# New PSUM banks and a new gate order in the first stage, and whole float32 copies for the 16-column products

## The reference, cut to what matters

```python
# first block (x is 512 x 1024, c is one condition vector)
sh1, sc1, g1, sh2, sc2, g2 = split(silu(c) @ ada_w + ada_b)      # ada_w is 1024 x 6144
u = rms_norm(x, mix_pre_g) * (1 + sc1) + sh1
y = concat_g((window_mean(u_g, w_g) - u_g) @ pool_w[g]) * pool_scale   # 4 groups of 256 columns
x = x + g1 * rms_norm(y, mix_post_g)
u = rms_norm(x, ffn_pre_g) * (1 + sc2) + sh2
x = x + g2 * rms_norm(conv_ffn(u), ffn_post_g)                   # u @ w_up (1024 x 5632), conv, gelu, @ w_down
# second block: two layers
p = x @ w_in                # gdn: q, k, v, gate, and 16 columns of b and a logits
x = layer_norm(a * x + gated_delta_rule(...) @ w_out)
p = x @ w_in                # gla: q, k, v, gate, and 16 columns of low rank gate input
x = layer_norm(a * x + gla_chunked(...) @ w_out)
```

## Time and profile before

| | |
|---|---|
| median of 3 runs | 1145.33 us (1144.76 to 1145.80) |
| profiled execution | 1145.01 us, span 1143.2 us |
| PE busy | 1123.7 us, 98% of the span |
| DVE, ACT, POOL busy | 548.4, 499.1 and 451.2 us |
| TensorE clock granted, mean | 0.996 of full speed |

### The profile page before, as it was taken

How to read it: one execution, slowest core, us unless ns; L and a number is a source line. 1 busy time by engine, 2 the same in 40 slices (tenths; PEclk the granted TensorE clock), 3 DMA queues, 4 the chain that set the end, 5 groups by cost and what they waited for, 6 DMA issues and landing times.

```text
span 1143.2 us, 17115 instructions
## 1 busy us (share of the span) xinstructions
PE 1123.7 (98%) x6826; PEld 916.5 (80%) x6826; DVE 548.4 (48%) x882; ACT 499.1 (44%) x692; POOL 451.2 (39%) x346
## 2 busy tenths in 40 slices
PE   8989999999999999999999999999999999999997
PEld 5658888888888888888788878888888888888886
DVE  3672554324452234567986556422200443676825
ACT  3374453544421223875443255744322343534632
POOL 0115544545445471654432211035354444564430
PEclk8999999999999999999999999999999999999999
DMA  9993232332342333433232211122343322223201
GB/s 343 415 384 111 74 110 82 101 110 73 110 128 78 111 111 112 148 110 112 75 108 78 75 37 38 74 74 74 108 125 109 111 79 91 95 75 111 75 1 74
DMA packets 87240, 128.97 MB, mean 113 GB/s; under 512 B 13300, under 2 KB 66306, under 8 KB 86919
## 3 DMA queue, kind: packets, MB, share of 16 engines
q1 hardware_dynamic: 81730, 119.62, 31.0%
q10 hardware_dynamic: 5445, 8.42, 2.1%
HBM read 122.77 MB, written 5.26 MB: 112 GB/s over the span
## 4 chain that ended last, share of the span: by engine, by line
PE 85%; DVE 5%; issue 3%; DMA 2%; ACT 2%; SPq 1%; POOL 1%; DVEq 0%; POOLq 0%
PE ps L295 24%; PE ps L297 24%; PE ps L296 24%; PE ps L1804 3%; DVE conv_v L1339 2%; DMA ada<-in_ada_w 1%; PE ps L2344 1%; DVE diag L1389 1%; PE ps L2345 1%; PE ps L2413 1%; PE ps L2403 1%; POOL wl L443 1%; PE ps L2350 1%; DVE outer L1386 1%; DVE shift_acc L1107 1%
## 5 line engine op out<-in xcount | busy, mean ns | idle before, releaser
L443 POOL TENSOR_TENSOR wl<-raw,wh 128x512 fp32r<-128x512 f32 x312 | 420.5, 1380 | 612.5 <-ACT wh L494 612.5
L295 PE MATMUL ps<-xth,wh 128*128 128x512 f32 (+1 forms) x832 | 324.4, 390 | 1.8 <-DVE xtl L1236 1.4
L297 PE MATMUL ps<-xth,wl 128*128 128x512 f32 (+1 forms) x832 | 317.4, 382 | 0.0
L296 PE MATMUL ps<-xtl,wh 128*128 128x512 f32 (+1 forms) x832 | 317.3, 381 | 0.0
L494 ACT ACTIVATE wh<-raw 128x2048 fp32r<-128x2048 f32 x78 | 149.3, 1914 | 304.9 <-PE ps L297 284.7
L295 PEld LDWEIGHTS ps<-xth,wh 128*128 128x128 f32 x832 | 156.5, 188 | 34.6 <-issue 4.5
L297 PEld LDWEIGHTS ps<-xth,wl 128*128 128x128 f32 x832 | 156.4, 188 | 30.4
L296 PEld LDWEIGHTS ps<-xtl,wh 128*128 128x128 f32 x832 | 156.7, 188 | 28.7 <-issue 0.5
L1244 DVE SCALAR_TENSOR_TENSOR conv_out<-ps,conv_taps,conv_out 128x511 f32<-128x511 f32 x44 | 32.8, 745 | 124.8 <-ACT conv_out L665 124.8
L1339 DVE SCALAR_TENSOR_TENSOR conv_v<-ps,gdn_taps,conv_v 128x511 f32<-128x511 f32 (+2 forms) x96 | 71.8, 748 | 40.2 <-ACT conv_v L733 37.5
L295 PE MATMUL ps<-wh,xth 128*128 128x512 f32 x176 | 69.7, 396 | 0.0
(11 more groups left out here) (368 smaller groups left out, 1628.1 us busy)
## 6 DMA issues: line engine op xcount, KB each, us to landing
ada<-in_ada_w SPq DMA_DIRECT2D x24, 1024.0 KB, 12.8
raw<-in_gdn_w_in SPq DMA_DIRECT2D x24, 1024.0 KB, 5.2
raw<-in_ffn_w_up SPq DMA_DIRECT2D x22, 1024.0 KB, 4.9
raw<-in_gla_w_in SPq DMA_DIRECT2D x12, 1024.0 KB, 5.0
raw<-in_ffn_w_down SPq DMA_DIRECT2D x11, 1024.0 KB, 4.9
raw<-in_gdn_w_out SPq DMA_DIRECT2D x8, 1024.0 KB, 4.9
raw<-in_gla_w_out SPq DMA_DIRECT2D x4, 1024.0 KB, 5.1
xres<-in_x SPq DMA_DIRECT2D x4, 512.0 KB, 5.3
```

What stands on the lines that cost most here:

```text
L295: nc.tensor.matmul(o, lh, rh, start=first, stop=False)
L296: nc.tensor.matmul(o, lh, rl, start=False, stop=False)
L297: return nc.tensor.matmul(o, ll, rh, start=False, stop=last)
L443: rest = nc.gpsimd.tensor_tensor(lo[:, part], raw[:, s, part], hi[:, part].bitcast(f32), ALU.subtract)
```

## The change

In the first stage the banks of y rotate as 2, 4, 6, 2 where they were 4, 6, 2, 4, and those of the turned tiles as 4, 6, 2, 4 where they were 6, 2, 4, 6. The first y tile is copied by ACT into SBUF (`first_mixed`), so that DVE works on it there and tile 3 may take its banks. The order of the programs of PE, DVE and ACT changes with it, some waits are taken at other places, four products of ones are put between the vector rows, two behind `mod_col`, and the four ahead of the up projection go. The second half of the second gain is summed between the first channel tiles, and the up unit runs both its halves for each channel tile instead of four tiles at a time. In the two `first_unit` stages ACT writes a third copy of each turned tile, `xt_whole`, in plain float32, and `narrow` reads that alone. The diff, cut to its core:

```diff
+    xt_whole = [at("xt_gdn", PH + 72 * KB, [KD, T]), at("xt_gla", PH + 32 * KB, [KD, T])]
+    first_mixed = at("first_mixed", PH, [D])
...
         def mixed_bank(tt):
+            return (2, 4, 6, 2)[tt]
+        def turned_bank(tt):
             return (4, 6, 2, 4)[tt]
-        def turned_bank(tt):
-            return (6, 2, 4, 6)[tt]
...
 # ACT: parts_high
                 nc.scalar.activation(xth[:, :, tt * P:(tt + 1) * P], ..., ACT.Copy).then_inc(S("parts_hi"), 1)
+                if stage < 2:
+                    for half in (1, 0):
+                        if half == 0:
+                            act.wait_ge(S("parts_lo"), parts_count(stage, tt, 2) + 1)
+                        nc.scalar.activation(xt_whole[stage][:, 4 * half:4 * half + 4, tt * P:(tt + 1) * P],
+                                             ps[:, b + half, :]..., ACT.Copy).then_inc(S("parts_hi"), 1)
...
 # ACT: first stage
-            for tt in range(2):
-                norm_square("y", tt)
-                norm_root("y", tt)
+            norm_square("y", 0)
+            norm_root("y", 0)
+            act.wait_ge(S("pool_in"), 34)
+            nc.scalar.activation(first_mixed[:], bank2(mixed_bank(0)), ACT.Copy).then_inc(S("act_ready"), 1)
+            norm_square("y", 1)
+            norm_root("y", 1)
...
-            nc.scalar.activation(ada_part[:, 1, :], ps[:, 1, :], ACT.Copy).then_inc(S("ada_summed"), 1)
...
-            norm_scale(3)
...
+            act.wait_ge(S("turned"), 4)
+            nc.scalar.activation(pooled[:, 4:KD, 3 * P:T], ps[:, turned_bank(3) + 1, :]..., ACT.Copy)...
...
 # DVE: parts_low in two halves, each behind ACT's copy of the other half
+                if stage < 2:
+                    for half in range(2):
+                        v.wait_ge(S("parts_hi"), parts_count(stage, tt, 3) + 1 + half)
+                        V.tensor_tensor(xtl[:, k, cols], ps[:, b + half, :]..., xth[:, k, cols].bitcast(f32), ALU.subtract)...
...
 # DVE: first stage
             norm("y", 1)
+            v.wait_ge(S("vec_mm"), 3)
+            V.tensor_tensor(g1_row[:, 0:512], ps[:, 0, :], post1_row[:, 0:512], ALU.mult)...
             v.wait_ge(S("mod_mm"), 4)
-            V.tensor_tensor(g1_row[:], bank2(0), post1_row[:], ALU.mult)...
+            V.tensor_tensor(g1_row[:, 512:D], ps[:, 1, :], post1_row[:, 512:D], ALU.mult)...
...
             norm("u", 2)
+            ada_sum(3)
             turned_out(0)
             norm("u", 3)
+            V.tensor_scalar(xn[:, 3, :], xres[:, 3, :], stat[:, 2, 3:4], None, ALU.mult)...
             turned_out(1)
             gain_sum(0)
             mod_col(3, 1, SH2)
+            v.wait_ge(S("turned"), 4)
+            V.tensor_copy(pooled[:, 0:4, 3 * P:T], ps[:, turned_bank(3), :]...)...
             gain_col(0)
-            gain_sum(1)
-            turned_out(3)
...
+            modulated(2)
+            modulated_low(0)
+            modulated_low(1)
+            gain_sum(1)
+            modulated_low(2)
+            gain_col(1)
+            v.wait_ge(S("mods_done"), 6)
...
 # PE
                 mm.then_inc(S("vec_mm"), 1)
+                keep_busy(2, 5)
...
-            pe.wait_ge(S("vec_done"), 2)
-            for n in range(3):
-                ada_unit(1, n)
+            pe.wait_ge(S("vec_done"), 1)
+            ada_unit(1, 0)
+            ada_unit(1, 1)
             pool_block(0)
             pool_block(1)
+            ada_unit(1, 2)
+            pool_block(2)
+            pool_block(3)
             ada_unit(1, 3)
-            pool_block(2)
+            pe.wait_ge(S("vec_done"), 2)
             mod_col(1, 3, 0)
             mod_col(1, 3, 1)
-            for cb in range(3, KD):
-                pool_block(cb)
-            mixed(0)
+            keep_busy(2, 2)
+            pool_block(4)
+            pool_block(5)
+            mixed_group(0, 0)
+            pool_block(6)
+            mixed_group(0, 1)
+            pool_block(7)
+            mixed_group(0, 2)
+            mixed_group(0, 3)
             mixed(1)
+            mixed_group(2, 0)
+            mixed_group(2, 1)
...
             mixed_shift(0)
-            mixed_shift(1)
             ada_unit(2, 2)
             ada_unit(2, 3)
+            mixed_shift(1)
+            mod_row(2, 0)
             mixed_group(2, 2)
-            mod_row(2, 0)
             mixed_group(2, 3)
             mixed_shift(2)
+            mixed(3)
+            mixed_shift(3)
             ada_unit(3, 0)
             ada_unit(3, 1)
-            mixed(3)
-            mixed_shift(3)
+            turn_normed(0)
...
-            gain_turn(1)
-            pe.wait_ge(S("pooled_written"), 2)
-            keep_busy(4, 3)
...
-                for part in range(2):
-                    for sub in range(2):
+                for k in range(KD):
+                    if k == 2:
+                        gain_turn(1)
+                    pe.wait_ge(S("u_lo"), k + 1)
+                    for sub in range(2):
...
 # PE: narrow
-                    for x in (xth, xtl):
-                        for c in range(4):
-                            mm = X.matmul(ps[32 * c:32 * c + 32, b, cols], w[:, kk + c, :], x[:, kk + c, cols].bitcast(f32), ...)
+                    for c in range(4):
+                        mm = X.matmul(ps[32 * c:32 * c + 32, b, cols], w[:, kk + c, :], xt_whole[stage][:, kk + c, cols], ...)
```

More of the change, by code:

```diff
@@ L252, in cell_bank, with pool_bank, mixed_tile, gain_bank @@
             return (4, 5, 7)[m % 3]
+        def pool_bank(cb):
+            return 4 + (cb + 1) % 4
+        def mixed_tile(tt):
+            return first_mixed[:] if tt == 0 else bank2(mixed_bank(tt))
         def mixed_bank(tt):
+            return (2, 4, 6, 2)[tt]
+        def turned_bank(tt):
             return (4, 6, 2, 4)[tt]
-        def turned_bank(tt):
-            return (6, 2, 4, 6)[tt]
+        def gain_bank(half):
+            return (0, 6)[half]
+        def gain_cols_bank(half):
+            return (0, 7)[half]
+        def parts_count(stage, tt, each):
+            return each * (stage * TT + tt) if stage < 2 else each * 2 * TT + tt
         def keys_bank(c):
@@ L1227, in _, with modulated_low @@
             modulated(0)
[L1228 to L1236 removed]
+            def modulated_low(n):
+                v.wait_ge(S("pooled_done"), KD + n + 1)
+                V.tensor_tensor(xtl[:, n, :], pooled[:, n, :], xth[:, n, :].bitcast(f32), ALU.subtract).then_inc(S("u_lo"), 1)
+            modulated(2)
[5 more added lines that the diff above has]
+            v.wait_ge(S("mods_done"), 6)
+            modulated(4)
+            modulated_low(3)
+            modulated(6)
+            for n in range(4, KD):
+                modulated_low(n)
             def up_taps(i, s, sub):
@@ L1980, in _ @@
             ada_unit(2, 0)
-            mixed_group(2, 0)
             pe.wait_ge(S("mods_done"), 2)
@@ L2160, in turn_x3, with narrow @@
                 turn_tile(xres[:, tt, :], 2 * tt)
-            def narrow(b, w, part):
+            def narrow(b, w, stage, part):
                 cols = slice(part * 256, part * 256 + 256)
                 for kk in range(0, KD, 4):
-                    for x in (xth, xtl):
-                        for c in range(4):
-                            mm = X.matmul(ps[32 * c:32 * c + 32, b, cols], w[:, kk + c, :], x[:, kk + c, cols].bitcast(f32),
-                                          start=(kk == 0 and x is xth), stop=(kk > 0 and x is xtl))
+                    for c in range(4):
+                        mm = X.matmul(ps[32 * c:32 * c + 32, b, cols], w[:, kk + c, :], xt_whole[stage][:, kk + c, cols],
+                                      start=(kk == 0), stop=(kk > 0))
                 return mm
@@ L2179, in beta_gate @@
                     pe.wait_ge(S("padded"), 1)
-                mm = narrow(3, ba_w, part)
+                mm = narrow(3, ba_w, 0, part)
                 if part == 1:
@@ L2485, in gate_low @@
                     pe.wait_ge(S("padded"), 2)
-                mm = narrow(2, low_w, part)
+                mm = narrow(2, low_w, 1, part)
                 if part == 1:
```

103 lines of the change are left out of this document (51 added, 52 removed).

## The result

The changed kernel took 1150.74 us (median of 20 runs, 1145.60 to 1151.92) beside 1144.74 us (20 runs) of the kernel before: ratio 1.0043, 95% interval 1.0033 to 1.0052. Forecast were 1141.1 us and a range that ends at 1146.0. The 20 times form two groups, called heaps here: 8 lie at 1145.6 to 1148.0, 12 at 1150.6 to 1151.9. The mean granted clock is 0.992 to 0.995 in the first and 0.989 to 0.990 in the second; the runs of the kernel before have 0.993 to 0.999. The profiled execution took 1145.67 us with a span of 1143.9 and belongs to the lower heap.

What follows compares the result with a forecast made beforehand. PE, busy 98% of the span, was taken as the bound. First stage 1.7, stage 1 1.7 and stage 0 0.7 make 4.1 us below 1145.01, or 1140.9, forecast as 1141.1; 8-in-10 range 1138.9 to 1146.0.

Steps and rivals of the forecast that it cites:

- The clock between 15 and 22 us: First stage: the clock stays high, so gate units start at 18.7 us; taken as little better than even.
- The price of splitting the pairs: First stage: products of ones end the pairs' overlap, each pair 1.8 us; gate units start 2.0 us later.
- the case for low clock: Rival, first stage: clock falls as before, gate units at 22.4 us, 1144.4 us in all; chance 0.27.
- the clock falls and comes back late: Rival, first stage: low stretch lasts twice 6.67 us, another 3.2 us lost, 1147.6 us in all; chance 0.13.
- From the vector rows to unit 1, -1.7 us: First stage: the second up unit is split at 88.4 us instead of starting at 90.08, 1.7 us won.
- part one: The reordered first stage, forecast to win 1.7 us by the second up unit.
- The gap ahead of unit 1: Ahead of the second up unit: PE waits 2.5 us; the clock coming down there was named as a way to be wrong.
- Stage 0, -0.7 us: Halved 16-column products in stage 0: `ba_cols` delayed by DMA issues, `gate_sums` ends 0.7 us earlier, bounds -0.4 and -1.8.
- Stage 1, -1.7 us: Halved 16-column products in stage 1: last tile turned 0.9 us earlier, ACT's copies hidden, 1.7 us won.
- The sum: Whole kernel: 1.7 + 1.7 + 0.7 = 4.1 us below the profiled execution's 1145.01, giving 1140.9.
- part two: 16-column products from whole copies, in both stages: 1.7 us won in stage 1 and 0.7 in stage 0.

Runs made afterwards that it cites:

- a1: The changed kernel run once more, unchanged: 1148.31 us, ratio 1.0036 against the kernel before.
- a2: Kernel before with only the new first stage, 16-column products as before: 1149.49 us, ratio 1.0046.
- a4: Changed kernel with five products of ones added behind up unit 0, where PE waits for unit 1: 1147.94 us, ratio 1.0026.
- c4: Kernel before with its four one-row products replaced by four full 128-row products of ones, vector rows not computed: 1144.35 us, ratio 1.0005.
- c1: Changed kernel without products of ones between the pairs, with five ahead of up unit 1 and `alog_dt` loads issued with the masks: 1140.08 us, ratio 0.9957.
- b1: Changed kernel without the four products of ones behind the two pairs of one-row products: 1141.88 us, ratio 0.9980.
- b3: Changed kernel without the four products of ones between the vector rows, and with five in the gap ahead of up unit 1: 1141.92 us, ratio 0.9985.
- c3: Kernel before with only the new first stage, without its four products of ones: 1143.02 us, ratio 0.9989.
- a3: Kernel before with only the 16-column products made from the whole copies: 1143.71 us, ratio 0.9997.
- b4: Kernel before with the 16-column products from whole copies and the `alog_dt` loads issued early, with the masks: 1141.43 us, ratio 0.9975.
- b2: Kernel before with only the four products of ones added, two behind each pair of one-row products: 1150.89 us, ratio 1.0063.
- c2: Changed kernel with the four products of ones behind both pairs of one-row products instead of two behind each: 1144.26 us, ratio 0.9994.

## Why the prediction was wrong

**The clock between 15 and 22 us: wrong, and this was the chosen case.** I took it as staying high because about as much dense work stood ahead of it as before. It fell in the profiles of the changed kernel and of a1, a2 and a4, at 14.5 to 15.9 us. The first gate unit began at 19.67 and, in a1, at 22.92, not at 18.7; unit 1 came 0.06 us earlier and 5.97 later than before, not 1.7 earlier. The reason given for the old fall may hold (c4); the conclusion that two short products of ones between the pairs remove it did not.

**The price of splitting the pairs: right in kind, and its worst case called a rival.** The step that says the two pairs ran side by side and now come apart holds: 1.98 and 2.06 us in place of 1.99 for all four. I wrote the case for low clock with two prices, +1.6 us and +4.8 (gate units and tiles on top), and gave them 0.27 and 0.13. The second, "the clock falls and comes back late", is what the upper heap shows: low until 25.1 us and again at 35. Its time was 1147.6; the heap lies at 1151, as the gap and stage 0 come on top. That the second stretch belongs to the ones isn't shown: c1 has one without them, the same 2.4 us behind the wait for the gate sum. A mechanism that I could price so should have had the larger share: a fall at 15 us, where the old one was, meets the second pair in the new order. It met it in four of five profiles with the ones between the pairs.

**From the vector rows to unit 1, -1.7 us: right in kind for what is left of it, missed as it stood.** In the lower profile each step is about 1 us late: shift columns at 43.47 (42.7), last sum of x until 67.02 (66.0), `modulated` at 73.48 (72.5), first up product 75.66 (74.6), ACT's third `modulated` 79.48 (77.9), unit 1 at 90.02 (88.4); and all that although its one-row products began 1.0 us earlier than in the profile of before. Without the ones, part one wins 2.2 us of distance in b1 and 2.7 in b3 and c3, but 0.8 in c1.

**The gap ahead of unit 1: seen, and counted as nothing.** I put 2.5 us of waiting there (2.24 measured) and named it as what could prove me wrong, but left it out of the sum, since the wait of 2.08 us at 70.72 had cost no clock. One profile was too little for that: the same wait of 2.08 to 2.09 us cost no clock in a3 and b4 either, but in b2 and c4 the clock was low as the wait ended or 0.4 us later, for 3.4 us. Behind the new gap the clock is 0.52 for 3.4 us in the lower profile, for 1.67 us of time. Five of the six profiles that have the gap show it (c2 doesn't).

The prediction drew on the Trainium skill ("TensorE: Matmul & The Clock Gate", Part 3), which says that products with few rows run at the same time if they lie in different row groups. The runs agree: 8 records in 2.0 us together, 4 in 1.98 apart.

**Stage 0, -0.7 us: wrong sign, +0.94.** `ba_cols` came as worked out: 10.67 us behind the turn of tile 2 (10.45 forecast), and PE waited 1.32. The failed step is the next one, that the chain through `conv_v` ends at `gate_sums`. The last DMA issue was moved along with the others, and I counted its time on ACT only, not its landing. DVE's first step of the gates needs `alog_dt`; it stood at 457.92 and was released by PE:

```profile
457.92 0.19 DVE L1453 TENSOR_TENSOR ba_tmp<-ps,alog_dt 128x32 f32<-128x32 f32 x1 [6.19 <-PE ps L2190]
```

The load issued at 453.48 had landed at 457.4 at the latest (these loads took 3.4 to 3.9 us from issue to landing), half a microsecond ahead of that step. In the changed kernel the issue is at 456.45 and the landing 4.4 us later at most, at 460.9, 1.6 us behind PE's last product at 459.3. What had been just in time became the last to come. Behind PE's wait the clock fell as well, but not in a4 and b3, with the same loss.

**Stage 1, -1.7 us: right**, 1.72.

**The sum.** Part one alone, with its losses, was 1.0046 and not -1.7 us; part two 0.9997 and not -2.4. The term that was most wrong is the four products of ones: counted at 2 us of later gate units with the clock kept, measured at 6.4 to 7.2 us (b1 against a1 and the first comparison). The gap is worth about 1.7 (in the trace only), the loads 2.5 to 3.2 us by the ratios (b4 against a3, c1 against b3), 1.8 to 2.3 by the medians. With the three repaired, c1 is 4.3 us under the kernel before. That this is near the 4.1 of the prediction's sum is chance: in c1's profile part one gives 0.8 (forecast 1.7), stage 0 1.7 (0.7, and with its loads moved), stage 1 1.7.

## What to carry to other kernels

Before putting filler products somewhere, see what runs side by side there: filler costs its own time and ends the overlap of the small products around it. A transfer that is issued on a busy engine's queue and moves later must be followed to its landing and to who reads it; small constants belong at a place where nothing waits for them. A wait that a change creates on TensorE is to be priced with the low clock behind it, and one profile in which such a wait cost nothing doesn't free it of that price; a stretch of low clock that the profile already shows is to be laid over the new order, to see what it would then meet.

## What the runs showed of the hardware

- Whether the granted clock falls in the first stage, and when, differs between executions of one program: at 15.9 for 3.5 us, or at 14.9 for 10.2 and again at 35.4 for 3.4. One-row products meet it at 3.77 instead of 1.98 us. So one order of instructions gives heaps of times 3 to 5 us apart, and a single profile can be one of the good heap.
- Behind a wait of 2.24 us of TensorE the clock fell 1.0 us after work had begun again, for 3.4 us; so it did in five of six profiles with this wait, and in none of the three where products of ones fill it (a4, b3, c1). At a wait of 2.08 or 2.09 us it fell in two of five (b2 and c4, not before, a3 and b4), at its end or 0.4 us later. Behind a wait of 0.91 us (28.67 in the lower profile) it fell 2.2 to 2.4 us later in three of nine (a1, a4 and c1, at 35.4, 35.0 and 28.7). That the 0.91 us are the cause isn't shown.
- A small load's issue on ACT takes 0.6 to 0.9 us at a quiet time (b4, at 323 us) and 0.6 to 1.8 when it follows four large ones, and it lands 2.9 us after issue there, 3.3 to 4.5 here (all other profiles).
